# Two-block transformer forward pass: the meta columns move behind the tokens in the rows of the activation buffer

## The reference

```
h = concatenate([meta, x], axis=1)              # 16 + 256 rows
proj = rms_norm(h, norm_mix_g) @ w_in           # 2048 -> 6 x 2048
u, gb_in, gc_in, v_in, ga_lin, gbr_lin = split(proj)
pooled = trailing means of u over 2, 4, 8, 16 rows, minus u
y_a = (pooled @ pool_w) * pool_scale
y_b = (gb_in * causal_conv_of_3_taps(gc_in * v_in)) @ conv_out_w
h = h + (sigmoid(ga) * y_a + sigmoid(gbr) * y_b) @ w_o
h = h + (silu(hn @ gate) * (hn @ up)) @ w_down
return rms_norm(h, norm_final_g)[:, 16:]        # the meta rows are dropped
```

## Time and profile before

| | us |
|---|---|
| median of 3 runs | 2633.67 |
| lowest, highest | 2633.49, 2633.74 |
| the profiled execution | 2633.6 |
| its span, first to last instruction | 2631.8 |
| TensorE busy | 2620.6 |
| VectorE busy | 1572.1 |
| ScalarE busy | 1172.8 |

### The profile page before, as it was taken

One profiled execution on the slowest core, in us unless ns is written; L12 is line 12 of the kernel. 1 busy time (PEld: TensorE's weight loads), 2 busy tenths in 40 slices (PEclk: granted clock), 3 DMA queues, 4 the chain that ended last, 5 costly groups with the idle time before them and its releaser, 6 DMA issues.

```text
span 2631.8 us, 50881 instructions
## 1 busy us (share of the span) xinstructions
PE 2620.6 (100%) x21394; PEld 2558.4 (97%) x21394; DVE 1572.1 (60%) x1557; ACT 1172.8 (45%) x1259; POOL 0.8 (0%) x7
## 2 busy tenths in 40 slices
PE   9999999999999999999999999999999999999998
PEld 8989999999999999999999999999999989998997
DVE  6567765555555556795676666556755555555555
ACT  5346544434443444465333333444454434443444
POOL 0000000000000000000000000000000000000000
PEclk9999999999999999999999999999999999999999
DMA  8654655555555565556555555555555555555553
GB/s 294 196 168 145 208 189 192 195 193 192 191 192 193 191 199 194 180 203 199 176 178 189 181 189 180 198 188 199 197 193 192 194 195 191 194 197 194 191 193 128
DMA packets 254275, 503.33 MB, mean 191 GB/s; under 512 B 8130, under 2 KB 11652, under 8 KB 253988
## 3 DMA queue, kind: packets, MB, share of 16 engines
q1 hardware_dynamic: 252180, 497.61, 57.4%
q10 hardware_dynamic: 1952, 3.68, 0.4%
HBM read 498.37 MB, written 2.88 MB: 190 GB/s over the span
## 4 chain that ended last, share of the span: by engine, by line
PE 99%; DMA 0%; DVE 0%; ACT 0%; SPq 0%; issue 0%; DVEq 0%; ACTq 0%
PE ps L1368 49%; PE ps L1379 24%; PE ps L1397 4%; PE ps L1399 4%; PE ps L1398 4%; PE ps L1417 4%; PE ps L1426 4%; PE ps L1421 4%; PE ps L1405 0%; PE ps L1406 0%; PE ps L1407 0%; DMA xtok<-in_x_dram 0%; PE ps L1562 0%; PE ps L1561 0%; PE ps L1560 0%; PE ps L1484 0%
## 5 line engine op out<-in xcount | busy, mean ns | idle before, releaser
L821 DVE TENSOR_TENSOR lo<-raw,hi 128x1024 fp32r<-128x1024 f32 x940 | 1144.5, 1224 | 920.6 <-ACT hi L494 905.7
L494 ACT ACTIVATE hi<-raw 128x1024 fp32r<-128x1024 f32 x940 | 991.6, 1060 | 1243.5 <-PE ps L1379 935.8
L1368 PE MATMUL ps<-A,hi 128*128 128x256 f32 x7283 | 903.6, 277 | 0.0
L1368 PEld LDWEIGHTS ps<-A,hi 128*128 128x128 f32 x7283 | 861.0, 188 | 0.3
L1368 PE MATMUL ps<-B,hi 128*128 128x256 f32 x3962 | 491.3, 277 | 0.0
L1379 PE MATMUL ps<-A,lo 128*128 128x256 f32 x3648 | 488.0, 276 | 0.0
L1368 PEld LDWEIGHTS ps<-B,hi 128*128 128x128 f32 x3962 | 468.1, 188 | 0.1
L1379 PEld LDWEIGHTS ps<-A,lo 128*128 128x128 f32 x3648 | 447.4, 188 | 0.0
L1379 PE MATMUL ps<-B,lo 128*128 128x256 f32 x1984 | 265.3, 276 | 0.0
L1379 PEld LDWEIGHTS ps<-B,lo 128*128 128x128 f32 x1984 | 243.2, 188 | 0.0
L1398 PE MATMUL ps<-lo,B 128*128 128x512 f32 x336 | 130.8, 389 | 0.0
(11 more groups left out here) (243 smaller groups left out, 1196.8 us busy)
## 6 DMA issues: line engine op xcount, KB each, us to landing
raw<-in_w_in_dram SPq DMA_DIRECT2D x136, 1024.0 KB, 5.1
raw<-in_ffn_w_dram SPq DMA_DIRECT2D x132, 1024.0 KB, 5.1
raw<-in_w_gate_up_dram SPq DMA_DIRECT2D x88, 1024.0 KB, 5.0
raw<-in_w_down_dram SPq DMA_DIRECT2D x44, 1024.0 KB, 5.0
raw<-in_w_out_dram SPq DMA_DIRECT2D x16, 1024.0 KB, 5.1
raw<-in_pl_w_gate_dram SPq DMA_DIRECT2D x16, 1024.0 KB, 5.1
raw<-in_conv_out_w_dram SPq DMA_DIRECT2D x16, 1024.0 KB, 5.0
raw<-in_w_o_dram SPq DMA_DIRECT2D x16, 1024.0 KB, 5.0
```

The source lines that it names most:

```text
L494: act.activation(hi[:, slot % RING], raw[:, raw_slot, 2 * (slot % 2):2 * (slot % 2) + 2, :], ACT.Copy).then_inc(hi_ready, 1)
L821: dve.tensor_tensor(lo[:, slot % RING], raw[:, slot // 2 % RAWS, 2 * (slot % 2):2 * (slot % 2) + 2, :], hi[:, slot % RING], ALU.subtract). ...
L1368: pe.matmul(ps[:, b0 + m, 0:T], high(slot, kk, m), x, start=j == 0 and kk == 0 and part == 0, stop=False)
```

## The change

In B the high token columns come first (0 to 255), then the last two meta rows, high and low (`AHEAD_HI`, `AHEAD_LO`, columns 256 to 259), then the other fourteen, high and low (`REST_HI`, `REST_LO`, 260 to 287). The low token columns begin at column 320 (`LOW_AT`). The token layout begins at column 16. `r_row` and `vec2` are allocated behind `ones` instead of before B, so B begins 1472 bytes earlier.

The first and third lines of `with_meta` multiply columns 0 to 271 (conv) or 0 to 287 (u2) of a row: the tokens and, behind them, high and low meta columns at once. The second line multiplies the 256 low token columns alone. All write from PSUM column 0. In conv twelve of the 272 columns are not used. VectorE's evacuations read the meta products from behind the tokens, in one more instruction for cv and cg and two more for u2. ScalarE's split of the meta rows is two instructions. All other places only name the high and low halves of B separately, since they no longer adjoin.

```diff
 VT0 = META - 2
 BROW = 576
-TOKEN_AT = META + 16
+TOKEN_AT = 16
+LOW_AT = 320
 TV = TM - VT0
-LO_META = TM + T
+AHEAD_HI, AHEAD_LO, REST_HI, REST_LO = T, T + 2, T + 4, T + 4 + VT0
...
         A = sb("A", [P, KT, 2 * T], F32R)
-        r_row = sb("r_row", [P, TM])
-        vec2 = sb("vec2", [P, V2N])
...
         ones = sb("ones", [P, P])
+        r_row = sb("r_row", [P, TM])
+        vec2 = sb("vec2", [P, V2N])
...
-        B_halves = B[:, :, META:META + 2 * T]
-        B_token = B[:, :, TOKEN_AT:TOKEN_AT + 2 * T]
+        B_high, B_low = B[:, :, 0:T], B[:, :, LOW_AT:LOW_AT + T]
+        A_parts, B_parts = (A[:, :, 0:T], A[:, :, T:2 * T]), (B_high, B_low)
+        token_parts = B[:, :, TOKEN_AT:TOKEN_AT + T], B[:, :, TOKEN_AT + T:TOKEN_AT + 2 * T]
...
-                    given.mark(act.activation(B[:, :, 0:META], metaT[:, :, :], ACT.Copy))
+                    act.activation(B[:, :, AHEAD_HI:AHEAD_HI + 2], metaT[:, :, VT0:META], ACT.Copy)
+                    given.mark(act.activation(B[:, :, REST_HI:REST_HI + VT0], metaT[:, :, 0:VT0], ACT.Copy))
...
                 elif kind == "u2":
                     dve.wait_ge(pieces_used, end)
-                    dve.tensor_tensor(meta_low[:, :, VT0:META], ps[:, b0:b0 + 4, TM:TM + 2], row_of(r_row[:, VT0:META], MT), ALU.mult)
-                    dve.tensor_tensor(meta_low[:, :, 0:VT0], ps[:, b0:b0 + 4, TM + 2:TM + META], row_of(r_row[:, 0:VT0], MT), ALU.mult)
-                    dve.tensor_tensor(win_a[:, :, :], ps[:, b0:b0 + 4, 0:TM], row_of(r_row[:, :], MT), ALU.mult).then_inc(psum_free, 1)
+                    ahead_r, rest_r = row_of(r_row[:, VT0:META], MT), row_of(r_row[:, 0:VT0], MT)
+                    dve.tensor_tensor(meta_low[:, :, VT0:META], ps[:, b0:b0 + 4, AHEAD_LO:AHEAD_LO + 2], ahead_r, ALU.mult)
+                    dve.tensor_tensor(meta_low[:, :, 0:VT0], ps[:, b0:b0 + 4, REST_LO:REST_LO + VT0], rest_r, ALU.mult)
+                    dve.tensor_tensor(win_a[:, :, VT0:META], ps[:, b0:b0 + 4, AHEAD_HI:AHEAD_HI + 2], ahead_r, ALU.mult)
+                    dve.tensor_tensor(win_a[:, :, 0:VT0], ps[:, b0:b0 + 4, REST_HI:REST_HI + VT0], rest_r, ALU.mult)
+                    dve.tensor_tensor(win_a[:, :, META:TM], sums, Rm, ALU.mult).then_inc(psum_free, 1)
...
                 elif kind in ("cv", "cg"):
-                    dve.tensor_tensor(meta_low[:, :, VT0:META], ps[:, b0:b0 + 4, TV:TV + 2], row_of(r_row[:, VT0:META], MT), ALU.mult)
-                    dve.tensor_tensor(to[:, :, :], ps[:, b0:b0 + 4, 0:TV], row_of(r_row[:, VT0:TM], MT), ALU.mult).then_inc(psum_free, 1)
+                    ahead_r = row_of(r_row[:, VT0:META], MT)
+                    dve.tensor_tensor(meta_low[:, :, VT0:META], ps[:, b0:b0 + 4, AHEAD_LO:AHEAD_LO + 2], ahead_r, ALU.mult)
+                    dve.tensor_tensor(to[:, :, 0:2], ps[:, b0:b0 + 4, AHEAD_HI:AHEAD_HI + 2], ahead_r, ALU.mult)
+                    dve.tensor_tensor(to[:, :, 2:TV], sums, Rm, ALU.mult).then_inc(psum_free, 1)
...
             def with_meta(seg, g, j, slot, b0, n):
-                ahead = META if seg.reads[1] == "wide" else META - VT0
+                columns = T + 2 * META if seg.reads[1] == "wide" else T + META
...
-                        pe.matmul(ps[:, b0 + m, 0:ahead + T], high(slot, kk, m), B[:, 2 * j + kk, META - ahead:TM],
+                        pe.matmul(ps[:, b0 + m, 0:columns], high(slot, kk, m), B[:, 2 * j + kk, 0:columns],
...
-                        pe.matmul(ps[:, b0 + m, ahead:ahead + T + ahead], high(slot, kk, m), B[:, 2 * j + kk, TM:TM + T + ahead],
+                        pe.matmul(ps[:, b0 + m, 0:T], high(slot, kk, m), B_low[:, 2 * j + kk, :],
...
-                        last = pe.matmul(ps[:, b0 + m, 0:ahead + T], low(slot, kk, m), B[:, 2 * j + kk, META - ahead:TM],
+                        last = pe.matmul(ps[:, b0 + m, 0:columns], low(slot, kk, m), B[:, 2 * j + kk, 0:columns],
```

More of the change, by code:

```diff
@@ L454, in run @@
                                 evacuate(kind, G, end, b0, turn * len(seg.kinds) + g, first_tile(seg, turn, g), more,
-                                         B_token if seg.name.startswith("f2") else B_halves)
+                                         token_parts if seg.name.startswith("f2") else B_parts)
                                 assert left[0] == 0, (kind, left)
@@ L508, in wait_group, with high_parts @@
                 act.nop(nofuse=True)
-            def high_parts(buf, k, a, src, name, n=MT):
+            def high_parts(to, k, src, name, n=MT):
                 for i in range(n):
-                    last = act.activation(buf[:, bass.ds(k + i, 1), a:a + T], src(i), ACT.Copy, scale=gain(name, k + i))
+                    last = act.activation(to[0][:, bass.ds(k + i, 1), :], src(i), ACT.Copy, scale=gain(name, k + i))
                 return last
@@ L563, in evacuate @@
                     more()
-                    given.mark(high_parts(A, k, 0, lambda i: some(h, k + i, 1, 0, T), "ffn" if kind == "res_ffn" else "ffn2"))
+                    given.mark(high_parts(A_parts, k, lambda i: some(h, k + i, 1, 0, T), "ffn" if kind == "res_ffn" else "ffn2"))
                     ready.skip()
@@ L574, in evacuate @@
                     wait_alone(asked)
-                    given.mark(act.activation(some(A if kind == "cb" else to_b, k, 4, 0, T), work[:, :, :], ACT.Copy))
+                    given.mark(act.activation(some((A_parts if kind == "cb" else to_b)[0], k, 4, 0, T), work[:, :, :], ACT.Copy))
                     ready.skip()
@@ L746, in side @@
                         for i in range(2):
-                            last = act.activation(B_halves[:, 2 * hd + i, 0:T], ps[:, 6, i * T:(i + 1) * T], ACT.Copy, scale=small[:, 20 + i:21 + i])
+                            last = act.activation(B_high[:, 2 * hd + i, :], ps[:, 6, i * T:(i + 1) * T], ACT.Copy, scale=small[:, 20 + i:21 + i])
                         given.mark(last)
@@ L833, in free_sums, with low_parts @@
                 dve.wait_ge(psum_free, G + 1)
[L835 removed]
+            def low_parts(to, k, src, name, n=MT):
                 for i in range(n):
[L837 to L838 removed]
+                    last = dve.scalar_tensor_tensor(out=to[1][:, bass.ds(k + i, 1), :],
+                                                    in0=src(i), scalar=gain(name, k + i), in1=to[0][:, bass.ds(k + i, 1), :],
                                                     op0=ALU.mult, op1=ALU.subtract)
@@ L888, in evacuate @@
                     wait(given)
-                    ready.mark(low_parts(A, k, 0, lambda i: some(h, k + i, 1, 0, T), "ffn" if kind == "res_ffn" else "ffn2"))
+                    ready.mark(low_parts(A_parts, k, lambda i: some(h, k + i, 1, 0, T), "ffn" if kind == "res_ffn" else "ffn2"))
                 elif kind == "part":
@@ L917, in evacuate @@
                         more()
-                    finish_split(to_b if kind == "up" else A, k)
+                    finish_split(to_b if kind == "up" else A_parts, k)
                 elif kind == "cout":
@@ L1012, in times_gain, with finish_split @@
                 dve.tensor_tensor(x, x, row_of(gfin_row[:, bass.ds(gi * GC, GC)], 2), ALU.mult)
-            def finish_split(buf, k):
+            def finish_split(to, k):
                 given.skip()
                 wait(given)
-                ready.mark(dve.tensor_tensor(some(buf, k, 4, T, 2 * T), work[:, :, :], some(buf, k, 4, 0, T), ALU.subtract))
+                ready.mark(dve.tensor_tensor(some(to[1], k, 4, 0, T), work[:, :, :], some(to[0], k, 4, 0, T), ALU.subtract))
             def rsqrt(var, mid, r, src, scale, meanwhile=lambda: None):
@@ L1168, in side @@
                     wait(given)
-                    dve.tensor_tensor(B[:, :, LO_META:LO_META + 2], metaT[:, :, VT0:META], B[:, :, VT0:META], ALU.subtract)
-                    step(dve.tensor_tensor(B[:, :, LO_META + 2:LO_META + META], metaT[:, :, 0:VT0], B[:, :, 0:VT0], ALU.subtract))
+                    dve.tensor_tensor(B[:, :, AHEAD_LO:AHEAD_LO + 2], metaT[:, :, VT0:META], B[:, :, AHEAD_HI:AHEAD_HI + 2], ALU.subtract)
+                    step(dve.tensor_tensor(B[:, :, REST_LO:REST_LO + VT0], metaT[:, :, 0:VT0], B[:, :, REST_HI:REST_HI + VT0], ALU.subtract))
                 elif what == "first_ffn_rstd":
@@ L1245, in side @@
                         for i in range(2):
-                            last = dve.scalar_tensor_tensor(out=B_halves[:, 2 * hd + i, T:2 * T], in0=ps[:, 6, i * T:(i + 1) * T],
-                                                            scalar=small[:, 20 + i:21 + i], in1=B_halves[:, 2 * hd + i, 0:T],
+                            last = dve.scalar_tensor_tensor(out=B_low[:, 2 * hd + i, :], in0=ps[:, 6, i * T:(i + 1) * T],
+                                                            scalar=small[:, 20 + i:21 + i], in1=B_high[:, 2 * hd + i, :],
                                                             op0=ALU.mult, op1=ALU.subtract)
@@ L1345, in activations @@
             def activations(buf, layout):
```

(9 more changed lines are left out.)

20 lines of the change are left out of this document (10 added, 10 removed).

## The result

The changed kernel took 2645.89 us in the median (2645.59 to 2646.35), the kernel before 2633.67 beside it: 1.0046 times as long, with a 95% interval of 1.0035 to 1.0057. The profiled execution has a span of 2644.1 us, 12.3 more. The forecast was 2633.3, and the range ended at 2637.9.

What follows compares the result with a forecast made beforehand. The prediction took TensorE's issue time to bound the kernel. Convolution +0.4 us and pooled path -0.7 us summed to -0.3 us, with nothing charged elsewhere: 2633.3 us, range 2627.6 to 2637.9.

Steps and rivals of the forecast that it cites:

- What bounds the kernel: Whole kernel: TensorE, busy 2620.6 of 2631.8 us, sets the end; 0.1 us of its issue is 0.1 us of time.
- r_row and vec2 only move: Allocation of these two tiles: their new place was charged nothing.
- The 256-column run is known: Middle line of with_meta: its eight 256-column matmuls take 0.907 us, as in plain pieces.
- r = 0.990: Changed lines of with_meta: eight 272-column matmuls starting on the 256-byte phase take 0.990 us.
- A: Rival on products over 256 columns: 6.7 ns paid once, columns otherwise; +4.25 us, 2637.9 us; chance 0.32.
- B: Rival on products over 256 columns: price in steps of 16 columns; -5.1 to -6.0 us, 2627.6 to 2628.5; chance 0.27.
- 0.053 us more for 288: Pooled path, first and third lines: eight 288-column matmuls cost 0.053 us more than eight of 272.
- The covers: VectorE and ScalarE work behind changed groups: delays hidden, tightest 3.0 us against 0.17; no charge, 2.6 us if gone.
- C: Rival on with_meta's products: columns alone count, 0.417 ns each; +7.2 us, 2640.8 us; chance 0.03.
- anything else: Whole kernel: the remaining outcomes, with a cover gone as the example; chance 0.02.

Runs made afterwards that it cites:

- e1: Changed kernel with r_row and vec2 allocated directly behind B, so h, pb_copy, work, ident and ones keep their earlier addresses: 2637.35 us, 1.0014 times the kernel before.
- e3: Changed kernel with one product split in 128 + 128 columns behind each of the two side steps: 2637.89 us, 1.0015 times the kernel before.
- e9: Changed kernel with the earlier side-tile addresses put back, plus the first product of each middle run split in 128 + 128 columns: 2645.96 us, single run.
- e4: Changed kernel with 260 instead of 272 columns in the first and third convolution products: 2640.99 us, 1.0028 times the kernel before.
- e2: Kernel before without its three split products in f1_up0 (pieces 8 to 10): 2665.43 us, single run.
- e5: Changed kernel with B's low token columns from column 304 instead of 320, 64 bytes ahead of the phase: 2667.28 us, 1.0128 times the kernel before.

## Why the prediction was wrong, point by point

**What bounds the kernel** held. TensorE's issue time sets the end to 0.1 us.

**"r_row and vec2 only move"** was the step that failed, with 8 of the 12 us. I looked for what the changed addresses do to the products that read B and found the phase kept. I did not ask what reads the tiles that moved along, h and ones. They are read by only 20 side products in the two steps concerned, but these set the rate of 77 pieces behind them. The trace of before held the evidence. The eight low products at 1.11 us ahead of a split and 1.07 behind it are in the fence above, and L1366 stands in the code with no other use in sight. I took the run of 256, 0.907 us, for a constant of the shape, from pieces that all lay in a fast stretch. Putting the addresses back takes the 8 us away (e1), and so does ending the state (e3).

**"The 256-column run is known"** failed for the same reason in the changed pieces. The middle run took 0.94 us in the convolution and 0.93 in the pooled path, not 0.907, because the wide products ahead of it leave the slower rate (e9; in the pooled path in every other piece). That is 0.034 x 64 + 0.026 x 32 = 3.0 us.

**r = 0.990** was right: the first and third convolution runs are 0.987 and 0.992 us from start to start, off 1.014 (A) and 0.960 (B). The row with the size and the start of the changed products was the one to take.

**0.053 us more for 288** was mis-sized: 1.067 and 1.061 us are 0.075 above 0.99. Twice 0.021 over 32 pieces is 1.3 us. Together with the middle run this turns the forecast's -0.3 us into the measured +4.1 for the two segments. (The forecast's own terms, +0.45 and -0.64, give -0.2; nothing hangs on it.)

**The covers** held. The tightest place of the changed kernel, VectorE and TensorE behind the first cg group:

```profile
1426.58 3.50 DVE L824 TENSOR_TENSOR lo<-raw,hi 128x1024 fp32r<-128x1024 f32 x3
...
1430.75 1.07 PE L1386 MATMUL ps<-B,lo 128*128 128x256 f32 x8
```

The first split ends near 1427.8, 2.9 us ahead of its use, 0.05 less than in before. TensorE waits for nobody between 1200 and 1700 us.

**The rivals.** A's +4.25 us for the two segments is near the measured +4.1, but that is luck and not A's mechanism. 272 columns cost what the forecast said, and from 260 to 272 the price rises by 3.3 to 4.5 ns, where A's columns would make it 5.0. B's steps of 16 fall with e4. C's mechanism, a middle run that gives back less than its share, points the right way (the run fell from 0.960 to 0.94, to 0.953 by C, to 0.907 by the forecast), but for another reason and in another size. None of them held the 8 us: what I gave 0.02 as "anything else" was the case.

## What to carry to other kernels

Before a price per instruction is called a constant, read it start to start in every stretch of the trace, above all behind short steps of another kind; where the same instruction has two prices, ask what sets it and what ends it. When a tile is moved, list every tile whose address moves along and who reads it; e1 kept the layout and avoided the 8 us by putting the moved tiles where they fill the gap. An odd instruction with no visible purpose in a tuned kernel may be holding a state: three of them were worth 31.6 us here.

## What the runs showed of the hardware

A stream of 256-column products with a weight load each runs at 113.3 or at 117.8 ns a matmul at the same granted clock of 0.999. It stayed at the slower rate for 848 us in e2. It changes rate at float32 side products, depending on where these have their operands: a shift by 1472 bytes decided it for `ones` behind the sums, and for h and ident behind the transposes, with opposite sign for `ones` at two steps. It returned to the fast rate at a product split in two in each of the places tried, and it can change at products over 256 columns. Moving operands that start 64 bytes off the phase slowed 17 of the 24 products of a piece, of which 8 read them (e5). A split in 128 + 128 columns costs about a full slot more: a plain piece of the changed kernel with a split takes 2.85 us and not 2.72.

The price above 256 is not one line: 258 to 260 columns 119.5 to 120.4 ns, 272 on the phase 123.4 to 124.0, 274 126.7, 288 132.6 to 133.4. What happens inside TensorE in the slower rate stays open; no run here shows it. Only one shift was tried for the side products' tiles and one for the low half of B. So which other starts are good or bad, and whether 256 bytes is the length that counts, is open as well.
